# Spreading the first GDN weight tiles evenly among the indexer's logits

## The reference

```python
logits = jnp.einsum('bqhd,bsd->bqhs', qib, k_idx_f)              # 8 heads of 64
score = jnp.einsum('bqh,bqhs->bqs', wb * IDX_HEADS ** -0.5, jax.nn.relu(logits))
y = w[0] * xp[:, 0:L]
for j in range(1, CONV_K):
    y = y + w[j] * xp[:, j:j + L]                                # then silu
```

## Time and profile before

| | us |
|---|---|
| median of 3 runs | 2362.06 (2359.44 to 2362.19) |
| the profiled execution | 2360.91 |
| its span | 2359.1 |
| TensorE matmul busy | 2258.7 (96% of the span) |
| VectorE busy | 1144.7 (49%) |
| ScalarE busy | 1012.5 (43%) |
| GpSimd busy | 1123.9 (48%) |

### The profile page before, as it was taken

One profiled execution on the slowest core, in us unless ns is written; L12 is line 12 of the kernel. 1 busy time (PEld: TensorE's weight loads), 2 busy tenths in 40 slices (PEclk: granted clock), 3 DMA queues, 4 the chain that ended last, 5 costly groups with the idle time before them and its releaser, 6 DMA issues.

```text
span 2359.1 us, 32723 instructions
## 1 busy us (share of the span) xinstructions
PE 2258.7 (96%) x12724; PEld 1848.5 (78%) x12724; DVE 1144.7 (49%) x2148; ACT 1012.5 (43%) x2249; POOL 1123.9 (48%) x824
## 2 busy tenths in 40 slices
PE   6999998999999999999989999989999999999997
PEld 5677877788778888888866778877887888888886
DVE  3768776444433344440146687765445233444302
ACT  5455545455532433332265455545455234333222
POOL 4265365234355555554442664453333555555542
PEclk9999999999999999999989999999999999999998
DMA  4212211222233333333322111212222333333332
GB/s 140 58 50 56 58 51 37 61 74 77 68 93 96 97 94 98 95 98 98 94 67 58 50 50 54 59 33 67 76 77 68 96 97 94 98 95 98 98 96 83
DMA packets 98506, 183.34 MB, mean 78 GB/s; under 512 B 10928, under 2 KB 11056, under 8 KB 98224
## 3 DMA queue, kind: packets, MB, share of 16 engines
q1 hardware_dynamic: 98352, 181.26, 26.9%
HBM read 179.12 MB, written 2.10 MB: 77 GB/s over the span
## 4 chain that ended last, share of the span: by engine, by line
PE 83%; DVE 8%; ACT 5%; POOL 2%; issue 1%; DMA 0%; SPq 0%; DVEq 0%; ACTq 0%; POOLq 0%
PE bank L1377 81%; PE bank L1443 2%; DVE z_act L913 1%; ACT w_hi L547 1%; POOL w_lo L456 1%; POOL mt_even L495 1%; DVE conv_acc L913 1%; DVE left L913 1%; PE bank L1688 1%; DVE ob_lo L910 1%; ACT k_sq L650 1%; ACT decay L658 1%; DVE inv L910 0%; DVE bank L910 0%; DVE left L1065 0%
## 5 line engine op out<-in xcount | busy, mean ns | idle before, releaser
L456 POOL TENSOR_TENSOR w_lo<-w_raw,w_hi 128x512 fp32r<-128x512 f32 x668 | 926.6, 1409 | 1155.7 <-ACT w_hi L547 1155.7
L1377 PE MATMUL bank<-xn_hi,w_hi 128*128 128x512 f32 x1936 | 784.6, 405 | 14.9 <-DVE conv_acc L913 6.0
L1377 PE MATMUL bank<-xn_hi,w_lo 128*128 128x512 f32 x1936 | 786.0, 406 | 0.0
L1377 PE MATMUL bank<-xn_lo,w_hi 128*128 128x512 f32 x1936 | 772.8, 399 | 0.4 <-POOL xn_lo L524 0.4
L547 ACT ACTIVATE w_hi<-w_raw 128x512 fp32r<-128x512 f32 x668 | 385.0, 624 | 669.6 <-PE bank L1377 662.7
L1377 PEld LDWEIGHTS bank<-xn_hi,w_hi 128*128 128x128 f32 x1936 | 369.2, 191 | 98.1 <-issue 10.7
L1377 PEld LDWEIGHTS bank<-xn_hi,w_lo 128*128 128x128 f32 x1936 | 368.6, 190 | 78.5 <-issue 7.3
L1377 PEld LDWEIGHTS bank<-xn_lo,w_hi 128*128 128x128 f32 x1936 | 368.9, 191 | 73.7 <-issue 1.5
L910 DVE TENSOR_TENSOR residual<-residual,bank 128x512 f32<-128x512 f32 x32 | 21.9, 684 | 258.5 <-PE bank L1377 258.4
L1377 PE MATMUL bank<-mid_hi,w_hi 128*128 128x512 f32 x352 | 136.9, 389 | 0.0
L1377 PE MATMUL bank<-mid_lo,w_hi 128*128 128x512 f32 x352 | 136.9, 389 | 0.0
(11 more groups left out here) (250 smaller groups left out, 3283.0 us busy)
## 6 DMA issues: line engine op xcount, KB each, us to landing
w_raw<-w_tiles SPq DMA_DIRECT2D x668, 256.0 KB, 2.6
residual<-x_t SPq DMA_DIRECT2D x4, 512.0 KB, 5.4
out_t<-normalised SPq DMA_DIRECT2D x8, 256.0 KB, 2.2
rope<-rope SPq DMA_DIRECT2D x1, 1024.0 KB, 10.4
mats<-mats SPq DMA_DIRECT2D x1, 704.0 KB, 7.8
vecs_all<-vecs SPq DMA_DIRECT2D x1, 133.0 KB, 7.7
```

The lines of the kernel that those rows point to most:

```text
L456: nc.gpsimd.tensor_tensor(w_lo[j][:], w_raw[j][:], w_hi[j][:].bitcast(F32), ALU.subtract).then_inc(s_lo, 1)
L1377: return nc.tensor.matmul(out, lhsT, rhs, start=start, stop=stop)
```

## The change

In TensorE's loop over the logits the 24, 8 and 8 products before u = 4, 16 and 20 become three products before each of u = 4 to 19, 48 in all: tile 2 lies before u = 4 to 11, tile 3, now whole, before u = 12 to 19. `issue(first_pair.products - first_pair.n - 36)` behind the loop is 60 products in place of 68. On ScalarE the wait for tile 2 and its `w_hi_after` go from u = 8 to u = 14, in front of the first tap of tile 2, which itself goes from u = 12 to u = 14. On VectorE the three taps of tile 2 go from u = 14, 16, 18 to u = 16, 18, 20.

```diff
                 for u, (t, i) in enumerate(IR):
-                    if u == 8:
-                        tile_done(l, T0_GDN + 2)
-                        w_hi_after(l, T0_GDN + 2)
                     if u == 10:
                         front_tanh(l, 0, 1)
-                    if u == 12:
-                        front(l, 0, 2, False, split_next=False)
+                    if u == 14:
+                        front(l, 0, 2, False)
...
-                                    12: [(1, "silu")], 14: [(2, "t0_")], 16: [(2, "t1_")], 18: [(2, "t2_")]}.get(u, []):
+                                    12: [(1, "silu")], 16: [(2, "t0_")], 18: [(2, "t1_")], 20: [(2, "t2_")]}.get(u, []):
...
                 for u, (t, i) in enumerate(IR):
-                    if u == 4:
-                        d.issue(3 * KD)
-                    if u in (16, 20):
-                        d.issue(KD)
+                    if 4 <= u < 20:
+                        d.issue(3)
                     if u >= 4:
                         pe.wait_ge(idx_a.sem, idx_a.after(l, "relu%d_%d" % IR[u - 4]))
```

## The result

The changed kernel takes 2375.6 us (median of 4 runs, 2373.4 to 2376.5) against 2362.1 before: a ratio of 1.0059, 95% interval 1.0047 to 1.0072. It is 13.5 us slower; forecast were 2376.5 and a range of 2366 to 2383. Run again on another occasion it took 2373.9 (ratio 1.0054, 1.0041 to 1.0068).

What follows compares the result with a forecast made beforehand. Tile 5's start was taken to follow VectorE's finish of the 24th logit: 2 x (5.15 later + 2.1 clock) = 14.5 us on the median 2362.06 gives 2376.5 us, range 2366 to 2383.

Steps and rivals of the forecast that it cites:

- A round trip: TensorE's loop: going from full-height products to half-height logits and back costs 0.40 us, bounds 0.20 and 0.45.
- The rival of the half-priced round trip: TensorE's loop: the change of height costs half, E comes 3.1 us earlier; 2370.4, or 2366.2 with clock held; chance 0.11.
- Broken pairs: TensorE's loop: each logit stands alone between products, half the rows idle, taking two records: 0.44, 0.64 or 0.86 us.
- the rival of a VectorE fed more evenly: Loop: VectorE sets the pace, its 4.5 us of idles end; 2357.3, chance 0.07.
- The sum for the loop: VectorE finishes the 24th logit at 105.4 against 100.25, 5.15 us later in each layer.
- a wait that the forecast had argued away: TensorE's loop: the ReLU of u-4 is not late, since TensorE's turn outlasts VectorE's logit and half a tap.
- The fifteen turns: TensorE's loop, u = 4 to 18: turns of 1.52, 1.72 and 1.94 us, 25.7 us together.
- VectorE's tail: VectorE after TensorE's logit 19 at T: last accumulations and one moved tap (0.67) end at T + 5.4 us.
- The edits on ScalarE and VectorE: Moved taps and weight split in the loop cost nothing, hidden by TensorE's long turns; the last tap adds 0.67 us to the tail.
- Tile 4 waits 0.5 us, tile 5 about 3.5: TensorE behind the loop: new 0.5 us wait before tile 4; wait before tile 5 grows from 1.7 to about 3.6 us.
- The clock in the loop: TensorE's loop has no idle, so it counts at full clock, 1.00 from 72 to 101.
- The clock behind the loop: After the longer wait before tile 5, TensorE's clock falls to 1.2 GHz, costing 2.1 us a layer, ends 0 and 2.5.

Runs made afterwards that it cites:

- the full-height kernel: Changed kernel, with every logit a full-height product against a copy of the keys with zeros on the other half's rows; 2360.9 us, ratio 0.9997.
- the two kernels that differ only in the order of the heads: Changed kernel with six products before every second logit, 2359.9 us; the same with heads in order 0, 2, 4, 6, 1, 3, 5, 7, 2372.1 us.
- the loop with pairs on one half: Six products before every second logit, heads reordered so both logits of a pair mostly lie on one half of the array's rows; 2372.1 us, ratio 1.0049.

## Why the prediction was right

- **A round trip costs 0.40 us.** Right. It was read from pairs only; lone logits gave turns of 1.53, 1.73 and 1.95 for 1.52, 1.72 and 1.94. That this is the change of height, and not of the number format, the forecast assumed; the full-height kernel shows it. The rival of the half-priced round trip (2370.4) fell: it needed turns 0.2 us shorter. The forecast had weighed the Trainium skill's rule on weight loads pulled ahead of running matmuls ("TensorE: Matmul & The Clock Gate", section "Step-by-step: what each phase is for"). Between products the trace of the changed kernel agrees (the load for the product at 75.90 starts at 75.67, with the product before), across a change of height it doesn't (the load for the logit at 76.22 starts at 76.22).
- **Broken pairs cost a logit's full length.** Right for the size of one: 0.66 for 0.64 at 384 keys, by the two kernels that differ only in the order of the heads. In all they are 5.20 us a layer there, with 0.83 of it at the first four logits, which the changed kernel doesn't pay.
- **TensorE paces the loop, so the rival of a VectorE fed more evenly has no room.** Right: VectorE waited for most of the lone logits from the ninth on (0.3 to 1.5 us each).
- **The sum for the loop was 5.15 us a layer; measured 5.77.** Logit 19 ended 29.1 us after the first, not 28.6. Of this, 0.32 is a wait that the forecast had argued away: at u = 4 TensorE now comes with its logit after three products, not 24, and ReLU 0 was not done (0.32 idle at 73.17). The fifteen turns gave 0.01 each, and the last group of products was 0.1 longer than its 0.68, because the sum left out there what the way out of a logit adds to the first product. VectorE's tail took 5.45 for 5.4. The forecast's times by the clock of the trace, 105.4 for the first mask and 111.6 for tile 5, were met almost exactly (105.42 and 111.58), and that is luck: the loop started 0.60 us earlier than before for a reason outside the change.
- **The edits on ScalarE and VectorE are hidden, but for one tap in the tail.** Right: 2361.2 alone, and 0.66 us of tail.
- **Tile 4 waits 0.5 us, tile 5 about 3.5.** Right, 0.51 and 3.43.
- **The clock in the loop.** It stood at 1.00, as forecast. The reason given, that the new loop has no idle in it, is not enough: the loop with pairs on one half has none either, and the clock fell in it in layer 1.
- **The clock behind the loop, 2.1 us a layer.** The mechanism held: the clock fell in both layers. The size was too large for the median. In the profiled execution the falls behind tile 5 cost 6.12/2 + 3.39/2 = 4.8 us against 4.2 forecast, but of that only 0.29 + 1.27 = 1.6 us are left at the ends: other falls, at waits that the change doesn't touch, lay elsewhere or were shorter. In the medians 13.5 - 11.5 = 2.0 us remain for it and for everything else, and by the second measurement (12.3 us slower) only 0.8. That the total came within 1 us is in part luck, since two sizes that were off compensated each other: 10.3 + 4.2 forecast, 11.5 + 2.0 measured.

## What to carry to other kernels

Two matmuls on different halves of the array run side by side only if nothing of full height stands between them, and going from one height to the other and back costs 0.4 us here; so fill a dependent loop with dense work in lumps between pairs, not in thin slices between single instructions. Leave enough of the dense work behind the loop to cover the tail of the engine that finishes it. And when an edit makes room on the chain (here the masks), look at what will then stand beside the other user of a shared resource, because the wait may pass to it.

## What the runs showed of the hardware

- A change of height on TensorE costs about 0.2 us from full to half and 0.2 back at full clock (0.09 and 0.10 in front of the first record, 0.10 to 0.11 at it); fp32r products and fp32 logits of the same height follow each other with next to no gap (1.34 us for 0.68 + 0.64).
- The clock behind an idle of TensorE before tile 5 is not a matter of the idle's length alone. After waits of 1.7 to 1.9 us it never fell (5 of 5, over the profiled executions); after 2.2 to 2.9 us it fell in 2 of 9, and those two were at 2.22, while at 2.23 it stayed up once and at 2.9 twice; after 3.4 us it fell in 9 of 10, for 3.4 to 6.8 us. What decides between the cases is open.
- With lone half-height logits between products the loops kept the full clock, for 30.6 us in the changed kernel. Before the change, with waits of 0.4 to 0.5 us at the logits, the clock fell in the loop (0.51 for 6.90 us). With pairs on one half and no wait it fell in one layer and not in the other. So a loop without waits is not enough to be sure of the clock, and what decides is open.
